# Retention heads of a hybrid decoder step: reordered output projection, earlier splits of a weight unit, later growth of the sample states

## The chip, the cores and the metric

The kernel is one launch on one core of a Trainium2 chip. The metric is the device time in microseconds (us), the median of several executions. One more execution was profiled; all rows below come from that one. The engines are named as in the profile: PE multiplies matrices, PEld is its weight load, DVE works on vectors, ACT evaluates functions, POOL is the general-purpose engine, SP issues DMAs.

## The reference

A trunk of 2 layers works on 592 token columns: 16 meta tokens and 512 prompt tokens of one sequence, and 8 running sequences of 8 tokens each. Cut to what matters here:

```
for each layer:
    xn = rmsnorm(x)
    q, k, v, z_a, x_b, z_b, g_a, g_b = split(xn @ w_in)
    for each of 4 retention heads:                 # dk = 256, dv = 512
        q, k = rope(q), rope(k)
        o = (q k^T * decay) v + (q S) * decay       # prompt: causal; samples: with their own state S
        S_new = gamma^L * S + (k * decay)^T v       # 8 sample states and 1 prompt state, each 256 x 512
        o_a = group_norm(o) * silu(z_a)
    a = o_a @ w_a                                   # summed over the heads
    b = rglru(conv4(x_b)) * silu(z_b) @ w_b
    x = x + (sigmoid(g_a) * a + sigmoid(g_b) * b) @ w_o
y = rmsnorm(x)
```

All inputs and outputs are float32.

## The kernel before

Every engine has its own instruction stream, written out by hand; semaphores order them. A precise float32 product is made of three passes in the fp32r format: each operand is kept as a rounded part (`_hi`) and a remainder (`_lo`), and PE adds hi*hi, lo*hi and hi*lo (`three`, L1558 to L1560; `three_of`, L1623 to L1625, for tiles on the left side that are not weights, and for the values).

**The stream of weights.** The weights come as units of 128 x 1024 numbers (512 KB) in a ring of four slots. SP loads unit u when PE has finished unit u - 4 (`unit_done`). ACT makes `w_hi` of the unit (`split_hi`, L439), DVE makes `w_lo` from it (`split_lo`, L447). In step i of a head both split unit i + 3 of that head (`AHEAD`). Each head has 16 units: 0 to 3 are the columns of q and k, 4 to 7 those of the values, 8 to 11 those of z_a, and 12 to 15 the head's rows of w_a. Two of SP's loads stand behind other work in its queue: unit 10 behind the storing of a block of keys to a scratch buffer, unit 11 behind the same for the values.

**The ring of PSUM banks.** PE writes most of its results (called jobs) into four banks in turn. A job must wait until DVE or ACT has emptied the bank of the job four places earlier (`wait_bank`, `freed`). Jobs are listed in `phases`. Four further banks are outside the ring: two called `sums`, and `v_last` and `o_last`.

**A head** runs on PE in this order: the projections of q and k; the values (`values(0)` to `values(3)`, one call for each of four units; they go to all four banks of the ring, one per block of 128 tokens, and the block of the last 80 tokens to `v_last`); projection 8; the growth of the sample states (`grow`: the product k^T v of two sequences, into two of the banks outside the ring) between the two halves of projection 9 and around the scores; projection 10; the inner products; the prompt's state; four transposes `oT` 0 to 3 of the normalized output of four token blocks; the first half of projection 11; the transposes `oT` 4 of the last token block; the second half of projection 11; and then the product with w_a in 16 jobs `("wa", m)`, for 8 row blocks m and 2 halves of the columns (n = 0, 1). Each of these jobs has 12 matmuls: four parts c, three passes each.

DVE and ACT follow step by step (`i`). In step 7, when the values are done, ACT copies each bank to `vtok_hi` (L744 for the last 80 tokens, then L763 for the four banks), and DVE writes the remainder to `vtok_lo` and frees the bank (L1148, L1171). After that both split unit 10. In step 8 ACT computes a tanh of projection 8 (L733), DVE multiplies (`silu`, L1082), DVE adds the first growth to two states (`grow(0, 0)`, L1060, two instructions; PE's next growth waits for them, because it writes the same two banks), and both split unit 11.

At the end of a head, DVE makes `oa` for the four parts c (`gate`, L1229). ACT rounds it to `oa_hi` (L790). The remainder `oa_lo` of the first three parts over the first 512 tokens is POOL's (L594), the rest is DVE's (`low_oa`, L1225). The last token block is normalized apart (`normalize(4)`, L1219): DVE computes its variance between the gates of c = 0 and c = 1, POOL the power -1/2 of it (`power`, L546). POOL starts on `oa_lo` when this normalization is done:

```
                    power(slice(4, 5), P, hh * 2 + 2)
                    pool.wait_ge(on_ready, hh * 2 + 2)
                    for k in range(3):
```

The second half of `oa` in part 3 is the last thing that is made: it needs the second half of projection 11, ACT's tanh of it, `silu(11, (1,))`, a product, ACT's rounding and DVE's `low_oa(5)`. On PE, the first job with n = 1 waits for it in front of its part c = 3 (`oal_ready`, third value).

After the four heads of a layer the RG-LRU branch, the gates and the output projection follow; the change does not touch them.

Of the kernel before, what the change touches and what calls it, by code (L numbers as in the profile page):

```python
# [39 lines left out]
KT = D_MODEL // P  # L40
# [130 lines left out]
def phases():  # L171
    r = []
    for t in range(4):
        r += halves(("proj", t), 1)
    r += [(("apart", u), 1) for u in range(3)] + [(("v", j), j // 3) for j in range(4)]
    for t in range(8, 11):
        r += halves(("proj", t), 1)
        if t == 9:
            r += [(("score", n), 0) for n in range(len(SCORE_JOBS))]
    r += [(("inner", j), 0) for j in range(4)] + [(("state", c), 0) for c in range(2)]  # L180
    r += [(("oT", c), 0) for c in range(4)] + [((("proj", 11), 0), 0), (("oT", 4), 0), ((("proj", 11), 1), 1)]
    for m in range(0, 8, 2):
        r += [((("wa", m + i), n), n * i) for n in range(2) for i in range(2)]
    l = []
    for g in range(2):
        def apart(which):
            return [(("apart", g, which, gate, n), 0) for gate in range(2) for n in range(2)]

        for t in range(5):
            l += halves(("proj", g, t), 1)  # L190
        l += apart(0) + halves(("proj", g, 5), 1) + apart(1)
        for gate in range(2):
            l += halves(("gate", g, 3, gate), 0)
        l += apart(2)
    four = [x for t in range(4) for x in halves(("proj", t), 1)]
    b = []
    for m in range(8):
        b += halves(("wb", m), (12 * (m + 1)) // 8 - (12 * m) // 8)
    out = {}
    at = (0, 0, 0)  # L200
    for name, passes, units, jobs in (("R", HEADS, 16, r), ("L", 2, 12, l), ("GA", 2, 4, four), ("GB", 2, 4, four),
                                      ("B", 1, 12, b), ("O", 2, 4, four)):
        out[name] = Phase(at, passes, units, jobs)
        at = out[name].after
    return out, at
# [6 lines left out]
def trunk(nc, x_in, w_units, gate_w, packs, final_gain, consts, decay, state_ret,  # L212
# [7 lines left out]
    with ctx:  # L220
# [314 lines left out]
        def _(pool):  # L535
# [13 lines left out]
            for l in range(0, DEPTH):  # L549
# [7 lines left out]
                for h in range(0, HEADS):  # L557
# [31 lines left out]
                    pool.wait_ge(on_ready, hh * 2 + 2)  # L589
# [75 lines left out]
        def _(act):  # L665
# [48 lines left out]
            for l in range(0, DEPTH):  # L714
# [10 lines left out]
                for h in range(0, HEADS):  # L725
# [10 lines left out]
                    for i in range(11):  # L736
# [8 lines left out]
                        if i != 7:  # L745
                            split_hi(act, "R", l, h, i)
# [13 lines left out]
                        if i == 7:  # L760
# [4 lines left out]
                            split_hi(act, "R", l, h, i)  # L765
# [212 lines left out]
        def _(dve):  # L978
# [43 lines left out]
            for l in range(0, DEPTH):  # L1022
# [28 lines left out]
                for h in range(0, HEADS):  # L1051
# [36 lines left out]
                    for i in range(11):  # L1088
# [39 lines left out]
                        elif i == 9:  # L1128
                            silu(i, (0,))
                            grow(0, 1)  # L1130
                            silu(i, (1,))
                        elif i >= 8:
                            silu(i)
                            if i == 8:
                                grow(0, 0)
# [14 lines left out]
                        if i not in (7, 9):  # L1150
# [17 lines left out]
                        if i == 7:  # L1168
# [5 lines left out]
                            split_lo(dve, "R", l, h, i)  # L1174
# [71 lines left out]
                    for c in range(3):  # L1246
# [5 lines left out]
                        if c == 2:  # L1252
# [37 lines left out]
                    for two in range(KT // 2):  # L1290
                        for n, (a, b) in enumerate(cut(l)):
                            for m in (2 * two, 2 * two + 1):
                                name = (("wa", m), n)
                                wait_job(dve, "R", l, h, name)
                                if h == 0:
                                    dve.tensor_copy(acc[:, m, a:b], psum_of("R", name)[:, 0:b - a])\
                                       .then_inc(freed("R", name), 1)
                                else:
                                    dve.tensor_tensor(acc[:, m, a:b], psum_of("R", name)[:, 0:b - a], acc[:, m, a:b],
                                                      ADD).then_inc(freed("R", name), 1)  # L1300
                            if n == 0 and two % 2 == 0:
                                grow_four(two // 2)
                        split_lo(dve, "R", l, h, 12 + two)
# [250 lines left out]
        def _(pe):  # L1554
# [73 lines left out]
            for l in range(0, DEPTH):  # L1628
                for h in range(0, HEADS):
# [158 lines left out]
                    for two in range(KT // 2):  # L1788
                        i = 12 + two
                        wait_unit("R", l, h, i)  # L1790
                        for n, (a, b) in enumerate(cut(l)):
                            for m in (2 * two, 2 * two + 1):
                                name = (("wa", m), n)
                                wait_bank(pe, "R", l, h, name)
                                for c in range(4):
                                    if m == 0 and n == 0 and c < 3:
                                        pe.wait_ge(oapl_ready, hh * 3 + (c + 1))
                                    elif m == 0 and c in (0, 3):
                                        pe.wait_ge(oal_ready, hh * 3 + (1 if n == 0 else 2 if c == 0 else 3))
                                    ins = three(psum_of("R", name)[:, 0:b - a], i % RING, m % 2 * 4 + c,  # L1800
                                                oa_hi[:, c, a:b], oa_lo[:, c, a:b], c == 0, c == 3)
                                done("R", name, ins)
                            if n == 0 and two % 2 == 0:
                                grow_four(two // 2)
# [178 lines left out]
```

## Time and profile before

| | before |
|---|---|
| median of 3 runs | 1956.12 us (1955.78 to 1957.28) |
| the profiled execution, its own time | 1955.78 us |
| its span, from first to last instruction | 1954.0 us |
| granted TensorE clock, mean | 0.997 |
| PE busy | 1928.1 us (99% of the span) |
| PEld busy | 1800.4 us (92%) |
| DVE busy | 1182.3 us (61%) |
| ACT busy | 735.1 us (38%) |
| POOL busy | 239.1 us (12%) |

The profile gives busy time by engine, by groups of instructions, and the idle time in front of each group with what ended it. The timeline lists single instructions of an engine: start, duration, line, tile written and tiles read, and in brackets the idle time before it and what ended that. Where the instructions of one tile are asked for, a row gives the shortest, median and longest duration in ns and the start of the first and the last, and for a DMA the us from its issue to its landing. An instruction of DVE or ACT may begin a little before the modelled end of the one in front of it.

### The profile page before, as it was taken

The page shows a single profiled execution, that of the slowest core. Times are in us where ns is not written, and L with a number is a line of the kernel's source. Part 1 is how long each engine was busy: PE and PEld are TensorE (multiplying, and loading weights), DVE is VectorE, ACT ScalarE, POOL GpSimd, SP SyncE. Part 2 cuts the span into 40 slices and gives each one's busy share as a digit, 9 for nine tenths or more (in the row PEclk, how much of TensorE's full clock was granted, in tenths as well). Part 3 has the DMA queues.
Part 4 walks back from the last instruction along what each step waited for, and adds up shares of the span by engine and source line. Part 5 has one row for each costly group of instructions (what it writes and reads, how often), then busy time and mean ns, then how long its engine had stood idle before and what let it go on. Part 6 is the DMA issues. An engine that isn't in the chain of part 4 may idle for free.

```text
span 1954.0 us, 32049 instructions
## 1 busy us (share of the span) xinstructions
PE 1928.1 (99%) x13176; PEld 1800.4 (92%) x13176; DVE 1182.3 (61%) x2021; ACT 735.1 (38%) x1136; POOL 239.1 (12%) x360
## 2 busy tenths in 40 slices
PE   8999999999999999999999999999999999999997
PEld 7789898898899999999988888988988999999997
DVE  7665565565666887424486655656647668863345
ACT  4332322322326776422333223223223367754222
POOL 1021120120232210000001201202102322000000
PEclk9999999999999999999999999999999999999999
DMA  6334534543453333322245345434534533332222
GB/s 214 123 123 162 166 123 124 171 150 115 133 159 103 99 102 111 124 77 76 87 169 161 119 132 172 159 97 142 189 105 142 162 103 105 101 127 85 82 83 79
DMA packets 105567, 247.00 MB, mean 126 GB/s; under 512 B 10798, under 2 KB 51102, under 8 KB 105038
## 3 DMA queue, kind: packets, MB, share of 16 engines
q1 hardware_dynamic: 78446, 149.74, 24.7%
q0 software_dynamic: 26976, 95.22, 14.6%
q8 instruction: 104, 1.70, 0.4%
q14 instruction: 41, 0.34, 0.1%
HBM read 186.10 MB, written 49.12 MB: 120 GB/s over the span
## 4 chain that ended last, share of the span: by engine, by line
PE 82%; DVE 7%; ACT 5%; ACTq 2%; DVEq 1%; issue 1%; DMA 1%; SPq 0%
PE bank L1558 19%; PE bank L1560 19%; PE bank L1559 19%; PE bank L1623 5%; PE bank L1624 5%; PE bank L1625 5%; PE last L1639 2%; PE last L1623 1%; PE last L1625 1%; PE last L1624 1%; PE sums L1652 1%; DVE ct L1353 1%; DVE rr L1406 1%; ACT ii L860 1%; DVE w_lo L447 1%
## 5 line engine op out<-in xcount | busy, mean ns | idle before, releaser
L1558 PE MATMUL bank<-xn_hi,w_hi 128*128 128x296 f32 (+1 forms) x2432 | 727.3, 299 | 0.0
L1560 PE MATMUL bank<-xn_lo,w_hi 128*128 128x296 f32 (+1 forms) x2432 | 722.8, 297 | 0.0
L1559 PE MATMUL bank<-xn_hi,w_lo 128*128 128x296 f32 (+1 forms) x2432 | 721.8, 297 | 0.0
L1558 PEld LDWEIGHTS bank<-xn_hi,w_hi 128*128 128x128 f32 x2432 | 457.3, 188 | 6.9 <-issue 6.2
L1559 PEld LDWEIGHTS bank<-xn_hi,w_lo 128*128 128x128 f32 x2432 | 457.8, 188 | 0.4
L1560 PEld LDWEIGHTS bank<-xn_lo,w_hi 128*128 128x128 f32 x2432 | 456.8, 188 | 0.0
L447 DVE TENSOR_TENSOR w_lo<-w_raw,w_hi 128x1024 fp32r<-128x1024 f32 x245 | 298.7, 1222 | 183.8 <-ACT w_hi L439 176.7
L439 ACT ACTIVATE w_hi<-w_raw 128x1024 fp32r<-128x1024 f32 x245 | 257.7, 1055 | 358.3 <-DMA w_raw<-in_w_units 353.4
L1558 PE MATMUL bank<-oa_hi,w_hi 128*128 128x296 f32 (+1 forms) x512 | 153.7, 300 | 0.0
L1559 PE MATMUL bank<-oa_hi,w_lo 128*128 128x296 f32 (+1 forms) x512 | 151.9, 297 | 0.0
L1560 PE MATMUL bank<-oa_lo,w_hi 128*128 128x296 f32 (+1 forms) x512 | 151.7, 296 | 0.0
L1558 PE MATMUL bank<-ob_hi,w_hi 128*128 128x296 f32 (+1 forms) x384 | 114.0, 297 | 0.0
L1559 PE MATMUL bank<-ob_hi,w_lo 128*128 128x296 f32 (+1 forms) x384 | 113.9, 297 | 0.0
L1560 PE MATMUL bank<-ob_lo,w_hi 128*128 128x296 f32 (+1 forms) x384 | 113.8, 296 | 0.0
L1623 PE MATMUL bank<-w_hi,xn_hi 128*128 128x512 f32 x256 | 101.6, 397 | 0.0
L1624 PE MATMUL bank<-w_hi,xn_lo 128*128 128x512 f32 x256 | 101.3, 396 | 0.0
L1625 PE MATMUL bank<-w_lo,xn_hi 128*128 128x512 f32 x256 | 101.2, 396 | 0.0
L1558 PEld LDWEIGHTS bank<-oa_hi,w_hi 128*128 128x128 f32 x512 | 96.3, 188 | 3.9 <-issue 3.9
L1559 PEld LDWEIGHTS bank<-oa_hi,w_lo 128*128 128x128 f32 x512 | 96.3, 188 | 0.0
L1560 PEld LDWEIGHTS bank<-oa_lo,w_hi 128*128 128x128 f32 x512 | 96.3, 188 | 0.0
L571 POOL DMA_DIRECT2D out_ret_s<-S x64 | 45.8, 717 | 330.3 <-DVEq L1063 184.3
L1558 PEld LDWEIGHTS bank<-ob_hi,w_hi 128*128 128x128 f32 x384 | 72.2, 188 | 0.0
(272 smaller groups left out, 3004.5 us busy)
## 6 DMA issues: line engine op xcount, KB each, us to landing
w_raw<-in_w_units SPq DMA_DIRECT2D x216, 512.0 KB, 3.6
S<-in_state_ret POOLq DMA_DIRECT2D x64, 512.0 KB, 5.0
out_ret_s<-S POOLq DMA_DIRECT2D x64, 512.0 KB, 6.2
w_raw<-in_w_units SPq DMA_DIRECT2D x64, 256.0 KB, 3.2
vst<-v_scr SPq DMA_DIRECT2D x8, 512.0 KB, 4.0
out_ret_p<-Sp POOLq DMA_DIRECT2D x8, 512.0 KB, 6.1
v_scr<-vtok_hi SPq DMA_DIRECT2D x16, 160.0 KB
dec<-in_decay POOLq DMA_DIRECT2D x9, 264.0 KB, 5.0
```

The source lines that it names most:

```text
L439: act.activation(w_hi[:, n % RING, :], w_raw[:, n % RING, :], ACT.Copy).then_inc(unit_hi, 1)
L447: dve.tensor_tensor(w_lo[:, n % RING, :], w_raw[:, n % RING, :], w_hi[:, n % RING, :].bitcast(f32), SUB).then_inc(unit_lo, 1)
L571: pool.dma_start(dst, S[:, s, :, :]).then_inc(s_out[s], 16)
L860: ins = act.activation(dst[r0:r1, tile, :].rearrange("p (n t) -> p n t", n=2), both[r0:r1, :].rearrange("p (n t) -> p n t", n=2)[:, :, 0:H ...
L1353: dve.scalar_tensor_tensor(ct[:, 0:wide], xpad[:, t, j:j + wide], w(j), ct[:, 0:wide], MUL, ADD)
L1558: pe.matmul(ps, w_hi[:, slot, cols], x_hi, start=first, stop=False)
L1559: pe.matmul(ps, w_lo[:, slot, cols], x_hi, start=False, stop=False)
L1560: return pe.matmul(ps, w_hi[:, slot, cols], x_lo, start=False, stop=last)
L1623: pe.matmul(ps, left_hi, right_hi, start=first, stop=False)
L1624: pe.matmul(ps, left_lo, right_hi, start=False, stop=False)
L1625: return pe.matmul(ps, left_hi, right_lo, start=False, stop=last)
L1639: ins = pe.matmul(o_last[at:at + QUAD, :], qz[:, c, b * QUAD:b * QUAD + QUAD], S[:, s, c, :], start=(n < 4 and c == 0), stop=(n >= 4 and c ...
```

## The change

The change has five parts, all within a retention head.

1. The jobs of w_a are done in another order. Before: for each pair of row blocks, both blocks with n = 0, then both with n = 1. After: each row block with n = 0 and n = 1, then the next. `grow_four` stays behind two jobs in each case.
2. POOL no longer waits for `on_ready` before `oa_lo`.
3. DVE normalizes the last token block after the gate of c = 1, not of c = 2.
4. In step 7, ACT and DVE split unit 10 after the copy of the last 80 tokens' values and before the four copies that free the ring's banks.
5. In step 8, DVE no longer adds the first growth before it splits unit 11; it does so at the beginning of step 9, behind the split.

```diff
@@ phases
-    for m in range(0, 8, 2):
-        r += [((("wa", m + i), n), n * i) for n in range(2) for i in range(2)]
+    for m in range(8):
+        r += halves(("wa", m), m % 2)
@@ gpsimd
                     power(slice(4, 5), P, hh * 2 + 2)
-                    pool.wait_ge(on_ready, hh * 2 + 2)
@@ scalar
-                        if i != 7:
-                            split_hi(act, "R", l, h, i)
+                        split_hi(act, "R", l, h, i)
...
                                 act.activation(vtok_hi[:, j, :], v_bank(j)[:, :], ACT.Copy)\
                                    .then_inc(vth_ready, 1)
-                            split_hi(act, "R", l, h, i)
@@ vector
                         elif i == 9:
+                            grow(0, 0)
                             silu(i, (0,))
                             grow(0, 1)
                             silu(i, (1,))
                         elif i >= 8:
                             silu(i)
-                            if i == 8:
-                                grow(0, 0)
...
-                        if i not in (7, 9):
+                        if i != 9:
                             split_lo(dve, "R", l, h, i)
...
                             dve.drain().then_inc(vtok_ready, 1)
-                            split_lo(dve, "R", l, h, i)
...
-                        if c == 2:
+                        if c == 1:
                             dve.wait_ge(rsd_ready, hh * 2 + 2)
                             normalize(4).then_inc(on_ready, 1)
...
-                    for two in range(KT // 2):
+                    for m in range(KT):
                         for n, (a, b) in enumerate(cut(l)):
-                            for m in (2 * two, 2 * two + 1):
...
-                            if n == 0 and two % 2 == 0:
-                                grow_four(two // 2)
-                        split_lo(dve, "R", l, h, 12 + two)
+                        if m % 2:
+                            split_lo(dve, "R", l, h, 12 + m // 2)
+                        elif m % 4 == 0:
+                            grow_four(m // 4)
@@ tensor
-                    for two in range(KT // 2):
-                        i = 12 + two
-                        wait_unit("R", l, h, i)
+                    for m in range(KT):
+                        i = 12 + m // 2
+                        if m % 2 == 0:
+                            wait_unit("R", l, h, i)
                         for n, (a, b) in enumerate(cut(l)):
-                            for m in (2 * two, 2 * two + 1):
...
-                            if n == 0 and two % 2 == 0:
-                                grow_four(two // 2)
+                        if m % 4 == 0:
+                            grow_four(m // 4)
```

## Rows read from the trace of the kernel before

**Rows 1.** The page, busy time and share of the span.

```profile
PE 1928.1 (99%) x13176; PEld 1800.4 (92%) x13176; DVE 1182.3 (61%) x2021; ACT 735.1 (38%) x1136; POOL 239.1 (12%) x360
```

**Rows 2.** Waits of PE, whole span: us in total, times, longest.

```profile
PE bank L1558 <- DVE w_lo L1007: 9.3, 1, 9.3
PE last L1623 <- DVE xn_lo L1047: 3.9, 4, 1.5
```

**Rows 3.** Load of unit 10 (heads 0, 1, 4, 5): issue, landing.

```profile
L518 SPq DMA_DIRECT2D w_raw<-in_w_units x1: 478/478/478, 70.4 to 70.4; - x1
DMA to landing us min/median/max: 3.7/3.7/3.7
...
L518 SPq DMA_DIRECT2D w_raw<-in_w_units x1: 342/342/342, 205.9 to 205.9; - x1
DMA to landing us min/median/max: 3.6/3.6/3.6
...
L518 SPq DMA_DIRECT2D w_raw<-in_w_units x1: 479/479/479, 1039.9 to 1039.9; - x1
DMA to landing us min/median/max: 3.9/3.9/3.9
...
L518 SPq DMA_DIRECT2D w_raw<-in_w_units x1: 337/337/337, 1173.7 to 1173.7; - x1
DMA to landing us min/median/max: 5.0/5.0/5.0
```

**Rows 4.** Timeline, start of projection 8 (heads 0, 1, 4), DVE's first bank.

```profile
76.40 0.30 PE L1558 MATMUL bank<-xn_hi,w_hi 128*128 128x296 f32 x1
...
212.61 0.30 PE L1558 MATMUL bank<-xn_hi,w_hi 128*128 128x296 f32 x1
...
1045.39 0.29 PE L1558 MATMUL bank<-xn_hi,w_hi 128*128 128x288 f32 x1
...
73.06 0.69 DVE L1171 TENSOR_TENSOR vtok_lo<-bank,vtok_hi 128x512 fp32r<-128x512 f32 x1 [0.70 <-ACT vtok_hi L763]
```

**Rows 5.** Timeline, step 8 and PE's second growth, head 1; last row head 6.

```profile
219.33 0.42 ACT L733 ACTIVATE zz<-bank 128x296 f32<-128x296 f32 x1 [2.84 <-PE bank L1560]
219.64 1.05 ACT L439 ACTIVATE w_hi<-w_raw 128x1024 fp32r<-128x1024 f32 x1
...
220.16 1.40 DVE L1060 SCALAR_TENSOR_TENSOR S<-S,cst,sums 128x512 f32<-128x512 f32 x2
221.47 1.22 DVE L447 TENSOR_TENSOR w_lo<-w_raw,w_hi 128x1024 fp32r<-128x1024 f32 x1
...
223.11 0.50 PE L1652 MATMUL sums<-vst,kst 24*128 24x512 f32 x2
...
1322.99 1.06 ACT L439 ACTIVATE w_hi<-w_raw 128x1024 fp32r<-128x1024 f32 x1 [0.61 <-DMA w_raw<-in_w_units]
```

**Rows 6.** Timeline, end of head 0, POOL, DVE, ACT and PE.

```profile
122.34 0.56 POOL L546 TENSOR_TENSOR rstd_gn<-mv,minus_half 128x1 f32<-128x1 f32 x1 [9.57 <-DVE mv L1213]
124.70 3.79 POOL L594 TENSOR_TENSOR oa_lo<-oa,oa_hi 128x512 fp32r<-128x512 f32 x3 [1.80 <-ACT oa_hi L790]
...
122.18 1.63 DVE L1229 SCALAR_TENSOR_TENSOR oa<-bank,gn_half,zz 128x512 f32<-128x512 f32 x2
123.95 0.55 DVE L1219 TENSOR_SCALAR vo<-vo,mv,rstd_gn 128x512 f32<-128x512 f32 x1
127.98 0.84 DVE L1225 TENSOR_TENSOR oa_lo<-oa,oa_hi 128x296 fp32r<-128x296 f32 x1
130.62 0.47 DVE L1225 TENSOR_TENSOR oa_lo<-oa,oa_hi 128x296 fp32r<-128x296 f32 x1 [0.55 <-ACT oa_hi L790]
...
124.75 0.42 ACT L733 ACTIVATE zz<-bank 128x296 f32<-128x296 f32 x1 [0.22 <-PE bank L1560]
128.52 0.42 ACT L733 ACTIVATE zz<-bank 128x296 f32<-128x296 f32 x1 [0.19 <-PE bank L1560]
...
131.18 0.30 PE L1558 MATMUL bank<-oa_hi,w_hi 128*128 128x296 f32 x1
```

More of the change, by code:

```diff
@@ L1289, in _ @@
                         dve.wait_ge(x_stored, l * 16)
-                    for two in range(KT // 2):
+                    for m in range(KT):
                         for n, (a, b) in enumerate(cut(l)):
-                            for m in (2 * two, 2 * two + 1):
[L1293 to L1300, printed above, removed]
-                            if n == 0 and two % 2 == 0:
-                                grow_four(two // 2)
-                        split_lo(dve, "R", l, h, 12 + two)
+                            name = (("wa", m), n)
+                            wait_job(dve, "R", l, h, name)
+                            if h == 0:
+                                dve.tensor_copy(acc[:, m, a:b], psum_of("R", name)[:, 0:b - a])\
+                                   .then_inc(freed("R", name), 1)
+                            else:
+                                dve.tensor_tensor(acc[:, m, a:b], psum_of("R", name)[:, 0:b - a], acc[:, m, a:b], ADD)\
+                                   .then_inc(freed("R", name), 1)
+                        if m % 2:
+                            split_lo(dve, "R", l, h, 12 + m // 2)
+                        elif m % 4 == 0:
+                            grow_four(m // 4)
                 dve.drain().then_inc(r_done, 1)
@@ L1787, in _ @@
                     project("R", l, h, ("proj", 11), 11, (1,))
-                    for two in range(KT // 2):
-                        i = 12 + two
-                        wait_unit("R", l, h, i)
+                    for m in range(KT):
+                        i = 12 + m // 2
+                        if m % 2 == 0:
+                            wait_unit("R", l, h, i)
                         for n, (a, b) in enumerate(cut(l)):
-                            for m in (2 * two, 2 * two + 1):
[L1793 to L1802, printed above, removed]
-                            if n == 0 and two % 2 == 0:
-                                grow_four(two // 2)
+                            name = (("wa", m), n)
+                            wait_bank(pe, "R", l, h, name)
+                            for c in range(4):
+                                if m == 0 and n == 0 and c < 3:
+                                    pe.wait_ge(oapl_ready, hh * 3 + (c + 1))
+                                elif m == 0 and c in (0, 3):
+                                    pe.wait_ge(oal_ready, hh * 3 + (1 if n == 0 else 2 if c == 0 else 3))
+                                ins = three(psum_of("R", name)[:, 0:b - a], i % RING, m % 2 * 4 + c,
+                                            oa_hi[:, c, a:b], oa_lo[:, c, a:b], c == 0, c == 3)
+                            done("R", name, ins)
+                        if m % 4 == 0:
+                            grow_four(m // 4)
                 pe.wait_ge(grown_free, (l + 1) * (HEADS * 2 * DEC_BATCH) + 1)
```

## The prediction, made before the changed kernel ran

> **What bounds the kernel now.** I read the page's busy times first: PE is busy for 99% of the span, the next engine, DVE, for 61% [rows 1]. Then the waits of PE: the longest is 9.3 us at the very start, the next sum is 3.9 us in four waits for `xn_lo` [rows 2], and no line that the change touches is among them. So PE runs its list almost without a gap, in a fixed order. Any wait that the change adds to PE is added to the time, as nothing later gives it back; and there is next to no wait that it could remove. The question is therefore which of the five parts makes something late for PE. For this I read the timeline at three places of a head. All eight heads show the same pattern with distances equal to some hundredths of a us; only the landings of the weight units differ. Time lies at 0.2 us from a release by another engine to the start of the waiting instruction, as from the end of the normalization at 124.50 (123.95 + 0.55) to POOL's start at 124.70 [rows 6]; I use it for PE too, where the profile shows no such case near, with 0.05 and 0.3 us as bounds.
>
> **Part 4, unit 10 split before the values' banks are freed.** Projection 8 is the next job for the ring, and its first half needs the bank of the first value block. Before, ACT copies it, DVE takes the remainder from 73.06 to 73.75 and the bank is free 2.6 us before PE comes at 76.40 [rows 4]. After, ACT first waits for unit 10 to land, and DVE for ACT. From the landing: ACT starts its split, 1.06 us [rows 5]; DVE splits, 1.22 us, and takes the next instruction about 0.1 us before the modelled end (in head 1 the growth of 1.40 us from 220.16 is followed at 221.47, by 0.09 us early) [rows 5]; its first value bank costs 0.69 us [rows 4]; then 0.2 us to PE. With 0.1 us for the two handovers from DMA to ACT to DVE the chain is 1.06 + 1.13 + 0.69 + 0.2 + 0.1 = 3.2 us from landing to PE.
>
> - Head 0: issued 70.4, landed after 3.7, so 74.1 [rows 3]; PE could start at 77.3 in place of 76.40 [rows 4]: 0.9 us late.
> - Head 4: issued 1039.9, landed 1043.8 [rows 3]; PE at 1047.0 in place of 1045.39 [rows 4]: 1.6 us.
> - Head 1: issued 205.9, landed 209.5 [rows 3]; PE at 212.7 in place of 212.61 [rows 4]: 0.05 to 0.1 us. Heads 2, 3, 6 and 7 have the same distance of 6.7 us from issue to PE and landings of 3.5 or 3.6 us: 0 to 0.1 us each, I take 0.25 us for these five heads together.
> - Head 5 has the distance too, but its landing took 5.0 us [rows 3]: 5.0 + 3.2 - 6.7 = 1.5 us.
>
> The sum is 0.9 + 1.6 + 0.25 + 1.5 = 4.2 us. The landing times set the bounds: all at 3.5 us and the short release give 2 us, all of heads 1 to 7 at 5.0 us give some 12 us. ACT's own copy is no limit: it ends about 0.6 us after its split, before DVE has finished splitting. Behind DVE in this place stand the three other banks; projection 8's second half needs the second one 3.3 us later, and it takes 0.6 us more, so it is hidden. That unit 10 is split earlier brings nothing: it is used only after projection 9 and the scores.
>
> **Part 5, the first growth behind the split of unit 11.** In head 1 PE's second growth runs at 223.11 and writes the banks that DVE's first growth reads [rows 5]. Before, that one ended at 220.16 + 1.40 = 221.56, with 1.5 us to spare. After, the order is ACT's tanh at 219.33, its split at 219.64 to 220.69, DVE's split from 220.73, 1.13 us, and then the growth from 221.87, 1.40 us, to 223.27 [rows 5]; with 0.2 us to PE that is 223.47, so PE waits 0.35 us. In head 6 ACT stood idle for 0.61 us for unit 11 to land [rows 5], which comes on top. In heads 0 and 4 unit 11 is late as well, but by then PE and the tanh are late through part 4, by more than the landing is. The sum is 8 x 0.35 + 0.6 = 3.4 us; the bounds are 8 x 0.2 = 1.6 us and, if unit 11 lands as late as in head 6 everywhere, 8 x 1.0 = 8 us.
>
> **Part 1, the jobs of w_a.** The same products in the same number, and `grow_four` behind the same number of jobs, so the ring and DVE's work keep their times. What moves is the job (0, n = 1): from third, behind a growth, to second place. Its part c = 3 needs DVE's `low_oa(5)`. Before, the fourth part of the second job starts at 131.18, and `low_oa(5)` ends at 130.62 + 0.47 = 131.09 [rows 6]. So with nothing else changed PE would be held for 0 to 0.2 us in each head; the old order had a job and the growth, 2.1 us, as cover. What makes this chain later is now paid in full.
>
> **Parts 2 and 3, POOL without its wait and the early normalization.** After, POOL goes from `power`, which ends at 122.34 + 0.56 = 122.90, straight into `oa_lo` of c = 0, three instructions of 1.26 us [rows 6]. DVE's gate of c = 1 ends at about 122.93, the first of two in 1.63 us, and the normalization follows 0.14 us later, as now behind c = 2 (123.81 to 123.95) [rows 6]: at 123.07. POOL is then 0.1 us ahead and both work on SBUF. What this costs is shown by one row: `low_oa(3)`, with the same shape and work as the 0.47 us of `low_oa(5)`, took 0.84 us from 127.98, while POOL was busy until 124.70 + 3.79 = 128.49 [rows 6]; it ended 0.33 us after POOL. DVE stood still for nearly the whole overlap. Between this and no cost lies the range for the normalization, whose own row shows that 512 numbers took 0.55 us, quicker than the 0.75 us of a gate of that width [rows 6]. I take the held case: it ends at about POOL's 124.2 + 0.4 = 124.6 in place of 123.6, 1.0 us late. The Trainium skill, "SBUF — State Buffer", section "SBUF: two separate sides", says the same in a rule: GpSimd and a VectorE instruction with two SBUF inputs, or in a mode that uses both ports, take one port pair in turn, each for its whole instruction. By it POOL's head start of 0.1 us is what decides; the row of `low_oa(3)` agrees for two inputs, and no row shows it for the normalization.
>
> Held, the delay goes on: the gate of c = 2 ends at 125.3, not at 123.8, 1.5 us later. ACT rounds it and only then takes the tanh of projection 11, which began at 124.75 with 0.22 us idle before it [rows 6]; it moves to 125.9, 1.15 us later. DVE's `silu`, the gate of c = 3, the last block and ACT's rounding of it move by as much, and the second tanh, which had 0.19 us idle and waited for PE [rows 6], moves from 128.52 to about 129.4, by 0.85 us. `low_oa(5)` then ends at 131.9, and PE starts its fourth part at 132.1 in place of 131.18: 0.9 us in each head, 8 x 0.9 = 7.2 us for parts 1, 2 and 3 together. The transposes `oT` 4, which PE reached at 124.55 and could start at 124.8, are within these 0.9 us. Not held, the three parts cost 0 to 0.2 us per head, some 0.8 us in all. POOL's earlier end brings nothing: PE reaches the third part of the first job at about 129.1, POOL ended at 128.49.
>
> **The sum.** 4.2 + 3.4 + 7.2 = 14.8 us on the profiled execution's own 1955.78 us gives 1970.6 us. The median of the runs is 0.34 us above that execution, so I predict 1970.9 us, 0.76% more. A measurement of this kernel tells a change from none from about 0.2%, or 3.9 us.
>
> **The rivals.**
>
> - The normalization is not held (POOL comes later than DVE, or this instruction doesn't collide). For it: POOL is only 0.1 us ahead, by times of 0.1 us grain, and its gates with a PSUM input ran beside POOL undisturbed (`silu` in the same window). Against it: the row of `low_oa(3)`. Time: 4.2 + 3.4 + 0.8 = 8.4 us, 1964.5 us.
> - POOL keeps its turn over two instructions, since its three stand close together (3.79 us for three), and the normalization is held for 2.3 us. For it: no gap between them. Against it: `low_oa(3)` met only the last of the three, so nothing shows it. Each head is 1.26 us later: 14.8 + 10 = 25 us, 1981 us.
> - The loads of units 10 land otherwise, since all transfers shift a little. With the landings of heads 4 and 5 at 3.5 us, part 4 costs 2.3 us less and the time is 1968.6 us; this is inside the range.
> - The other side: PE is held for `on_ready` today. The normalization ends at 124.50 and the transposes come at 124.55, a distance of 0.05 us, which could be a release. The earlier normalization would then give up to 0.2 us per head, 1.6 us, and 1954.5 us. It decides only if parts 4 and 5 cost under 0.2 us per head, that is if DVE frees the value bank 3 us or less after unit 10 lands and the growth takes no place behind the split. Against it: the transposes stand in PE's rhythm, directly behind the matmul in front of them, and PE has no such wait in its list [rows 2].
>
> **How the numbers follow.** My forecast has a chance of 0.52, the first rival 0.27, the second 0.10, the other side 0.04; 0.07 is left for parts 4 and 5 well off their sums in either direction. The forecast's own range is 1967 to 1976 us. To hold 8 in 10 the range takes in the first rival: 1962.5 to 1977 us. Slower by over 0.2% 0.94, within 0.2% 0.05, faster 0.01.
>
> **What would show it.** In the profile of the changed kernel: PE's waits name DVE's L1171 (`vtok_lo`) in front of projection 8, long in heads 0, 4 and 5, near nothing elsewhere; DVE's L1060 in front of the second growth, 0.3 to 0.4 us in each head; and DVE's `low_oa(5)`, L1225, in front of a matmul with `oa_hi`, 0.9 us in each head. The normalization of the last block takes 1.5 us in place of 0.55, and `low_oa(3)` 0.47 us in place of 0.84. If it takes 0.55 us, the first rival is right. If PE shows no wait for L1171, the chain of part 4 is wrong, and if the span grows by more than PE's named waits, I have missed a place.

## The result and the profile after

The changed kernel takes 1966.9 us (median of 5 runs, 1965.73 to 1969.67), the kernel before 1955.78 us on the same chip (5 runs, 1955.32 to 1957.28). The medians are 11.1 us apart. The ratio of the runs is 1.0062, with a 95% interval of 1.0051 to 1.0074, which is 12 us. The profiled execution has a span of 1965.1 us, 11.1 us more than before, and the granted clock is 0.998.

The page of the changed kernel, busy times:

```profile
PE 1931.5 (98%) x13176; PEld 1799.6 (92%) x13176; DVE 1184.6 (60%) x2021; ACT 732.0 (37%) x1136; POOL 240.9 (12%) x360
```

The instructions are the same in number, and no engine has more work worth speaking of [rows 1]. What is new stands in the list of PE's waits (us in total, times, longest):

```profile
PE bank L1553 <- DVE w_lo L1004: 8.9, 1, 8.9
...
PE bank L1553 <- DVE vtok_lo L1167: 3.1, 3, 1.3
PE sums L1647 <- DVE S L1057: 2.6, 6, 1.0
...
PE bank L1553 <- DVE oa_lo L1220: 0.9, 4, 0.2
```

The first row was there before [rows 2]. The other three are the three places of the prediction: `vtok_lo` is the first value bank in front of projection 8, `S` the first growth in front of the second, `oa_lo` the last remainder in front of the fourth part of a w_a job. This list counts only what is left when the modelled end of the matmul in front is taken off; the whole of a wait is seen in the distance between two starts.

**Step 7.** Timeline of the changed kernel, head 0, ACT, DVE and PE; the last row is the start of projection 8 in head 5:

```profile
69.23 0.59 ACT L743 ACTIVATE vtok_hi<-last 80x512 fp32r<-80x512 f32 x1 [4.24 <-PE last L1620]
72.63 1.06 ACT L439 ACTIVATE w_hi<-w_raw 128x1024 fp32r<-128x1024 f32 x1 [2.80 <-DMA w_raw<-in_w_units]
73.60 2.04 ACT L761 ACTIVATE vtok_hi<-bank 128x512 fp32r<-128x512 f32 x4
...
73.72 1.23 DVE L447 TENSOR_TENSOR w_lo<-w_raw,w_hi 128x1024 fp32r<-128x1024 f32 x1 [3.18 <-ACT w_hi L439]
74.87 2.48 DVE L1167 TENSOR_TENSOR vtok_lo<-bank,vtok_hi 128x512 fp32r<-128x512 f32 x4
...
74.36 0.40 PE L1620 MATMUL bank<-w_lo,xn_hi 128*128 128x512 f32 x1
75.70 0.38 PE L1553 MATMUL bank<-xn_hi,w_hi 128*128 128x296 f32 x1 [0.94 <-DVE vtok_lo L1167]
...
1188.21 0.37 PE L1553 MATMUL bank<-xn_hi,w_hi 128*128 128x288 f32 x1 [1.30 <-DVE vtok_lo L1167]
```

ACT stands idle for 2.8 us until unit 10 lands, with a value bank ready to be copied; then everything follows in the new order, and PE starts projection 8 3.1 us after the landing. The last value matmul starts at 74.36 and projection 8 at 75.70, a distance of 1.34 us; it is 0.23 us where nothing is late. In heads 4 and 5 the distances are 1.27 and 1.69 us, in the five others 0.23 or 0.24. What a distance has above 0.23 us is the cost: part 4 costs 1.1 + 1.0 + 1.5 = 3.6 us in this execution.

**Step 8.** The same for head 1; the last two rows, one of ACT and one of PE, are of head 2:

```profile
219.59 0.42 ACT L732 ACTIVATE zz<-bank 128x296 f32<-128x296 f32 x1 [2.84 <-PE bank L1555]
219.91 1.05 ACT L439 ACTIVATE w_hi<-w_raw 128x1024 fp32r<-128x1024 f32 x1
...
220.99 1.23 DVE L447 TENSOR_TENSOR w_lo<-w_raw,w_hi 128x1024 fp32r<-128x1024 f32 x1 [0.48 <-ACT w_hi L439]
222.14 1.40 DVE L1057 SCALAR_TENSOR_TENSOR S<-S,cst,sums 128x512 f32<-128x512 f32 x2
...
223.59 0.50 PE L1647 MATMUL sums<-vst,kst 24*128 24x512 f32 x2 [0.15 <-DVE S L1057]
...
357.98 1.06 ACT L439 ACTIVATE w_hi<-w_raw 128x1024 fp32r<-128x1024 f32 x1 [0.83 <-DMA w_raw<-in_w_units]
...
361.67 0.50 PE L1647 MATMUL sums<-vst,kst 24*128 24x512 f32 x2 [0.98 <-DVE S L1057]
```

In head 1 the growth ends at 222.14 + 1.40 = 223.54 and PE goes on at 223.59. In head 2 unit 11 lands late, ACT is idle for 0.83 us, and PE waits 0.98 us; before, it was head 6 where it landed late [rows 5]. The distance from the matmul in front of PE's second growth to it is 0.45 us in heads 0, 1 and 3, 0.51 us in head 5 and 1.28 us in head 2, against 0.22 or 0.23 us before. In heads 4, 6 and 7 it is 0.70 to 0.76 us: there too ACT had to wait a little for unit 11 after its tanh, and PE goes on 3.7 us after the landing, as in head 2. Summed over eight heads the excess is 3.5 us, of which 2.0 us is the new order (0.22 us in each head of the first layer, 0.29 in the second) and 1.5 us the landings.

**The end of a head.** Head 0 of the changed kernel, POOL, DVE, ACT and PE:

```profile
121.86 0.56 POOL L546 TENSOR_TENSOR rstd_gn<-mv,minus_half 128x1 f32<-128x1 f32 x1 [9.57 <-DVE mv L1208]
122.39 2.71 POOL L593 TENSOR_TENSOR oa_lo<-oa,oa_hi 128x512 fp32r<-128x512 f32 x2
...
122.58 1.38 DVE L1214 TENSOR_SCALAR vo<-vo,mv,rstd_gn 128x512 f32<-128x512 f32 x1
123.88 0.74 DVE L1224 SCALAR_TENSOR_TENSOR oa<-bank,gn_half,zz 128x512 f32<-128x512 f32 x1
...
130.73 0.47 DVE L1220 TENSOR_TENSOR oa_lo<-oa,oa_hi 128x296 fp32r<-128x296 f32 x1 [0.55 <-ACT oa_hi L787]
...
125.24 0.40 ACT L732 ACTIVATE zz<-bank 128x296 f32<-128x296 f32 x1
...
124.06 0.61 PE L1780 MATMUL bank<-cst,vo 128*128 128x128 f32 x4
124.76 0.38 PE L1553 MATMUL bank<-xn_hi,w_hi 128*128 128x296 f32 x1
...
131.25 0.41 PE L1553 MATMUL bank<-oa_hi,w_hi 128*128 128x296 f32 x1
```

POOL starts its first remainder 0.19 us before DVE's normalization, and the normalization takes 1.38 us in place of 0.55 [rows 6]. It ends 0.28 us after POOL's first remainder, and POOL's second remainder takes 1.46 us in place of 1.29. PE is late twice. The last remainder ends at 130.73 + 0.47 = 131.20 and PE starts its fourth part at 131.25, 0.41 us behind the matmul in front of it (0.5 us in the second layer, 0.13 without a wait). The other place was not in the prediction: between the starts of the transposes `oT` 4 (124.06) and of the second half of projection 11 (124.76) lie 0.70 us. In the kernel before it was 0.41 us:

```profile
124.56 0.66 PE L1785 MATMUL bank<-cst,vo 128*128 128x128 f32 x4
124.97 0.38 PE L1558 MATMUL bank<-xn_hi,w_hi 128*128 128x296 f32 x1
```

That half of projection 11 goes into the bank of the transposes of c = 2, which the gate of c = 2 empties at 123.88 + 0.74 = 124.62. This gate stands behind the held normalization. So the end of a head costs 8 x 0.29 us there and 4 x 0.28 + 4 x 0.37 us in front of the fourth part; behind that second stop the next matmul also comes after 0.24 us in place of 0.14. Together that is some 5.7 us.

The three sums, 3.6 + 3.5 + 5.7 = 12.8 us, are 1.7 us more than the growth of the span. The beginning makes the difference: the last value matmul of head 0 starts at 74.36 here, and 1.8 us later in the kernel before (0.23 us in front of the 76.40 of [rows 4]); the change has nothing in front of it. Most of it is TensorE's clock. In the profiled execution of the kernel before, the granted clock was at its lower level for 3.4 us from 53.1 us on, which cost PE 1.6 us; in that of the changed kernel it was not. The stretch in the kernel before and in the changed kernel (us, PE, PEld, DVE, ACT and POOL busy, granted clock, DMA share, GB/s):

```profile
53.20:56.40 3.20, 3.20 (x9) 2.50 (x8) 2.57 (x4) 1.23 (x2) 0.00 (x0) 0.50 0.00 0
...
53.20:56.40 3.20, 3.20 (x16) 2.59 (x14) 2.57 (x5) 0.98 (x3) 0.00 (x0) 1.00 0.00 0
```

So the difference of these two spans understates what the change costs by 1.7 us.

### The profile page after: what moved, and what is told of

The parts are those of the page before. It is cut to its first block, busy times and chain, and to the rows that moved or that the text cites. A ratio compares the mean times of both kernels' runs of the same rounds, so it can differ in the third digit from the quotient of the medians.

```text
span 1965.1 us, 32049 instructions
## 1 busy us (share of the span) xinstructions
PE 1931.5 (98%) x13176; PEld 1799.6 (92%) x13176; DVE 1184.6 (60%) x2021; ACT 732.0 (37%) x1136; POOL 240.9 (12%) x360
## 4 chain that ended last, share of the span: by engine, by line
PE 68%; DVE 11%; ACT 7%; issue 4%; DMA 3%; DVEq 2%; ACTq 2%; SPq 1%; POOL 0%; POOLq 0%
PE bank L1553 17%; PE bank L1555 17%; PE bank L1554 17%; PE bank L1618 4%; PE bank L1620 4%; PE bank L1619 4%; DMA w_raw<-in_w_units 2%; DVE w_lo L447 1%; ACT w_hi L439 1%; DVE ct L1348 1%; PE last L1634 1%; PE sums L1647 1%; PE last L1618 1%; DVE rr L1401 1%; PE last L1620 1%
## 5 line engine op out<-in xcount | busy, mean ns | idle before, releaser
L1079 DVE SCALAR_TENSOR_TENSOR zz<-zz,bank 128x296 f32<-128x296 f32 (+1 forms) x64 | 29.3, 457 | 80.2 <-ACT zz L732 79.9
```

The costliest lines, as they stand in the source:

```text
L1079: dve.scalar_tensor_tensor(zz[:, i - 8, a:b], zz[:, i - 8, a:b], 1.0, psum_of("R", name)[:, 0:b - a], ADD, MUL)\
```

## The experiments

**Each part alone.** Three kernels split the change, a fourth takes the order of the w_a jobs by itself. They ran on one chip.

`e1_split10`, part 4 alone:

```diff
-                        if i != 7:
-                            split_hi(act, "R", l, h, i)
+                        split_hi(act, "R", l, h, i)
...                                                          # behind the four banks
-                            split_hi(act, "R", l, h, i)
...
-                        if i not in (7, 9):
+                        if i != 9:
                             split_lo(dve, "R", l, h, i)
...                                                          # behind the four banks
-                            split_lo(dve, "R", l, h, i)
```

> The kernel before with part 4 alone: unit 10 is split before the four value banks are freed. My theory (PE waits in front of projection 8 for the first value bank, because DVE stands in its queue behind unit 10): 4 us slower in all, with PE waits for DVE's vtok_lo of about 1.1 us in head 0, 1 to 1.6 us in head 4 and in any head where unit 10 lands after 5 us, and none elsewhere. Rival (the waits of the changed kernel at this place come from its other parts, through the ring or the loads): no more than 1 us slower and no wait for vtok_lo.

Measured: 1959.2 us, before 1956.47 us, ratio 1.0015 (1.0006 to 1.0024), 2.9 us. In the waits of PE, DVE's remainder of the value bank stands as in the changed kernel:

```profile
PE bank L1555 <- DVE vtok_lo L1169: 2.9, 3, 1.9
```

Projection 8 starts at 76.73 in head 0, 2.0 us late, 0.9 us late in head 4, 0.5 us in head 5, where the landing took 4.1 us this time, and 0.2 us in head 6, where it took 3.8 us. In the heads with a landing of 3.5 or 3.6 us and 6.7 us from issue to PE there is no wait. Head 0 is later than expected, and not by its landing: unit 10 was issued at 69.91, only 4.8 us before PE was due, against 5.8 us in the changed kernel, and landed after 3.7 us. The theory holds; the size follows the issue and the landing from execution to execution.

`e2_growth`, part 5 alone:

```diff
                         elif i == 9:
+                            grow(0, 0)
                             silu(i, (0,))
...
-                            if i == 8:
-                                grow(0, 0)
```

> The kernel before with part 5 alone: DVE splits unit 11 before it adds the first growth. My theory: PE waits in front of its second growth for DVE's first one, 0.2 to 0.5 us in most heads, and about 0.9 us in head 0 and 1.2 us in head 4, where unit 11 lands late and part 4 is not there to cover it; 4 to 5 us in all. Rival (unit 11's landing has no part in it, only the order of DVE counts): the same 0.2 to 0.5 us in all heads, 2 to 3 us in all.

Measured: 1960.78 us, ratio 1.0021 (1.0012 to 1.0031), 4.1 us.

```profile
PE sums L1651 <- DVE S L1060: 3.4, 6, 1.1
```

PE's second growth is 0.2 to 0.3 us late in five heads, 0.9 us in head 0, 1.1 us in head 4 and 1.0 us in head 6. So the landing of unit 11 counts where the delay of part 4 does not stand in front of it, as the theory had it. In the changed kernel the same waits are 0.2 us in head 0 and 0.5 us in head 4: the parts overlap there.

`e3_end`, parts 1, 2 and 3, and `e4_order`, part 1 alone (the diffs are those of the change).

> The kernel before with parts 1, 2 and 3: new order of the jobs of w_a, POOL without its wait, normalization behind the gate of c = 1. My theory: DVE's normalization of the last block is held by POOL's first remainder and takes 1.4 us in place of 0.55; PE pays twice, 0.3 us in front of the second half of projection 11 (bank of the transposes of c = 2) and 0.3 to 0.4 us in front of the fourth part of the second job of w_a; 5 us in all. Rival (the three parts cost only what my first sum had without the hold): 1 us or less.

> The kernel before with part 1 alone: the jobs of w_a in the order of the changed kernel. My theory: the last remainder of oa ends just before PE wants it, so PE waits less than 0.1 us per head, 0 to 0.6 us in all, within the noise. Rival (the old order was a cover that is already needed, so the order by itself costs): 0.2 us or more per head, 1.6 us or more in all, with a PE wait for low_oa in each head.

Measured: `e3_end` 1961.86 us, ratio 1.0028 (1.0018 to 1.0037), 5.5 us; `e4_order` 1956.37 us, ratio 1.0 (0.9991 to 1.0009). In the first one the normalization takes 1.38 us again, and PE's weight load waits in all eight heads (the row below); in the second one PE has no wait for `oa_lo`:

```profile
PEld bank L1557 <- DVE oa_lo L1224: 3.2, 8, 0.5
```

The three groups add up: 0.15% + 0.21% + 0.28% = 0.64%, the change has 0.62%. The new order costs nothing by itself.

**What holds the normalization.** `e5_end_old_order` has parts 2 and 3 with the old order, `e7_order_norm` has parts 1 and 3 with POOL's wait kept (`pool.wait_ge(on_ready, hh * 2 + 2)` back in its place).

> The kernel before with parts 2 and 3 but the old order of the jobs of w_a. My theory: the normalization takes 1.4 us, PE waits 0.3 us in front of the second half of projection 11, and the later wait is covered by the old order; 2 to 2.5 us in all. Rival (the two waits are one delay that PE meets wherever it comes first): 5 us, as with the new order.

> The kernel before with parts 1 and 3, POOL's wait kept. My theory: without POOL beside it the normalization takes 0.55 us in its new place too; 0 to 1 us slower than before, from a small wait for the last remainder. Rival (the place of the normalization, not POOL, costs the time): 3 us or more.

Measured: `e5_end_old_order` 1958.11 us, before 1956.46 us, ratio 1.0008 (0.9999 to 1.0017); `e7_order_norm` 1956.48 us, ratio 1.0 (0.9991 to 1.0008). With the old order the second of PE's two waits is gone and the first one stays, 0.29 us in each head in the trace; the time of the runs, 1.6 us, is just inside the noise (the interval takes in 1), and below the 2 us that were expected. With POOL's wait kept, the normalization is as quick as before in its new place. The groups of 40 normalizations, `e5_end_old_order` above and `e7_order_norm` below (busy us, mean ns):

```profile
L1218 DVE TENSOR_SCALAR vo<-vo,mv,rstd_gn 128x512 f32<-128x512 f32 x40 | 26.3, 709 | 10.4 <-POOL rstd_gn L546 9.3
```

```profile
L1219 DVE TENSOR_SCALAR vo<-vo,mv,rstd_gn 128x512 f32<-128x512 f32 x40 | 19.7, 545 | 10.4 <-POOL rstd_gn L546 9.3
```

So POOL is the cause, not the place: (26.3 - 19.7) / 8 = 0.83 us for each held normalization.

The trace of `e7_order_norm` also shows something small that the earlier place gives. From the start of the transposes `oT` 4, which read what the normalization writes, to the second half of projection 11 it takes 0.35 us in all eight heads, as in the three other kernels whose early normalization is not held by a remainder (`e9_dve_first`, `e10_dec_only`, `e12_repaired`). In the kernel before, and in the kernels with the normalization in its old place, it takes 0.41 us. That is 0.5 us for eight heads, which the times of the runs cannot tell from nothing.

**Who starts first.** Two kernels reverse the order of the two starts. In `e9_dve_first` POOL waits for the gate of c = 1, which puts it 0.1 us behind DVE; in `e6_end_dec_first` it issues the load of the next decay table before its remainders. Both have parts 1, 2 and 3.

```diff
                     power(slice(4, 5), P, hh * 2 + 2)
+                    pool.wait_ge(oa_ready, hh * PARTS + 2)                                       # e9_dve_first
...
                     power(slice(4, 5), P, hh * 2 + 2)
+                    pool.dma_start(dec[:, :], decay[ds(h + 1, 1)]...).then_inc(dec_in, 16)       # e6_end_dec_first
...
-                    pool.dma_start(dec[:, :], decay[ds(h + 1, 1)]...).then_inc(dec_in, 16)       # e6_end_dec_first
```

> The kernel before with parts 1, 2 and 3, and POOL starts its remainders only when DVE's gate of c = 1 is written, so that it comes about 0.1 us behind DVE's normalization. Theory of turns (who starts first keeps the SBUF port for its whole instruction): the normalization takes 0.55 us, POOL's first remainder takes some 0.3 us longer, 0 to 1 us slower than before in all. Rival (POOL wins whenever both are there): the normalization takes 1.4 us or more and the time is 5 us above before.

> The kernel before with parts 1, 2 and 3, and POOL issues the load of the next decay table (some 0.6 us) before its three remainders of oa in place of behind them, so that DVE's normalization starts first. My theory (POOL and DVE take turns by the instruction, and who starts first goes on): the normalization takes 0.55 us, gate c = 2 frees its bank in time, 0 to 1 us slower than before. Rival (both are slowed wherever they overlap, whoever starts first): the normalization takes 1 us or more and the cost stays at 3 us or more. Other rival (the normalization is slow in its new place whatever POOL does): 1.4 us, 5 us in all.

Measured: `e9_dve_first` 1955.66 us, before 1955.88 us, ratio 0.9996 (0.9987 to 1.0005). Its timeline, head 0, POOL and DVE:

```profile
121.63 4.08 POOL L594 TENSOR_TENSOR oa_lo<-oa,oa_hi 128x512 fp32r<-128x512 f32 x3 [0.27 <-DVEq L1249]
...
121.52 0.55 DVE L1219 TENSOR_SCALAR vo<-vo,mv,rstd_gn 128x512 f32<-128x512 f32 x1
```

DVE is 0.11 us ahead and is not held; now POOL pays, 4.08 us for its three remainders in place of 3.79 [rows 6]. So between these two instructions a head start of 0.1 or 0.2 us decides who waits.

`e6_end_dec_first` missed its expectation widely: 1984.96 us, before 1956.46 us, ratio 1.0144 (1.013 to 1.0158), 28.5 us. Timeline, head 0, POOL and DVE:

```profile
123.08 0.61 POOL L589 DMA_DIRECT2D dec<-in_decay  x1
123.71 2.50 POOL L594 TENSOR_TENSOR oa_lo<-oa,oa_hi 128x512 fp32r<-128x512 f32 x2
...
123.28 3.23 DVE L1218 TENSOR_SCALAR vo<-vo,mv,rstd_gn 128x512 f32<-128x512 f32 x1
```

The normalization, dispatched 0.2 us after POOL's issue of the DMA and 0.4 us before POOL's first remainder, ends at 126.51, 0.30 us after the second remainder. A reading that fits is that DVE was not first here: the issue of the DMA on POOL had taken the turn already, and the remainders behind it kept it. The Trainium skill, "SBUF — State Buffer", section "Who interferes with whom", has both halves: `tensor_scalar` can run in a mode with two ports, which cannot run beside a GpSimd instruction, and the writing of DMA descriptors by GpSimd needs a port too; whoever issues first keeps the pair for its instruction. The runs agree for a pair of single instructions; no run here shows which mode the normalization ran in, and that several instructions of POOL in a row go first is not in the rule.

`e10_dec_only` and `e11_dec_one` take this apart: in the first one only the DMA's issue runs beside the normalization, in the second one the issue and one remainder, then POOL waits. Both have parts 1 and 3; `e11_dec_one` has part 2 with the wait put behind the first remainder. The issue is moved, as in `e6_end_dec_first`.

```diff
+                    pool.dma_start(dec[:, :], decay[ds(h + 1, 1)]...).then_inc(dec_in, 16)
-                    pool.wait_ge(on_ready, hh * 2 + 2)           # kept in e10_dec_only
                     for k in range(3):
                         what = (slice(None),) + pieces(l)[k]
+                        if k == 1:                               # e11_dec_one alone
+                            pool.wait_ge(on_ready, hh * 2 + 2)
```

> The kernel before with parts 1 and 3 and POOL's wait kept, and POOL's issue of the decay table's load put in front of that wait. Only this issue runs beside the normalization now, no remainder. If POOL's issue of a DMA holds DVE as a remainder does: the normalization takes 0.7 to 0.9 us, it ends 0.3 us behind the issue, and the time is within 1 us of before. If it does not: 0.55 us, and the 3.2 us that the normalization took with the issue and two remainders behind it have another cause.

> The kernel before with parts 1, 2 and 3; POOL issues the decay table's load, does one remainder, waits for the normalization, and does the other two. Where the issue and two remainders stood in a row, the normalization took 3.2 us. If POOL keeps its turn while its instructions stand close together: 1.9 to 2.1 us here, ended by the wait. If the wait of the normalization is one stretch that does not depend on how many follow: 3 us, or a standstill. PE stops for 0.8 us per head instead of 1.8, TensorE keeps its clock, and the time is 10 to 16 us above before, not 28.

Measured: `e10_dec_only` 1956.21 us, before 1955.88 us, ratio 1.0001 (0.9992 to 1.001); `e11_dec_one` 1967.62 us, ratio 1.0057 (1.0044 to 1.0071), 11.7 us. The two timelines, head 0:

```profile
122.69 0.61 POOL L589 DMA_DIRECT2D dec<-in_decay  x1
...
122.90 0.63 DVE L1219 TENSOR_SCALAR vo<-vo,mv,rstd_gn 128x512 f32<-128x512 f32 x1
```

```profile
122.02 0.61 POOL L589 DMA_DIRECT2D dec<-in_decay  x1
122.65 1.29 POOL L596 TENSOR_TENSOR oa_lo<-oa,oa_hi 128x512 fp32r<-128x512 f32 x1
...
122.23 2.01 DVE L1220 TENSOR_SCALAR vo<-vo,mv,rstd_gn 128x512 f32<-128x512 f32 x1
```

With the issue alone the normalization ends 0.23 us behind it and takes 0.63 us (0.62 to 0.65 in the eight heads) in place of 0.55. That is between the two expected values; it speaks for a hold, of which 0.08 us shows because the normalization needs most of the time anyway. With one remainder behind the issue it takes 2.01 us and ends 0.30 us after that remainder, with two 3.23 us. The hold grows by one remainder each time, which speaks for turns that POOL keeps. But in the changed kernel the normalization came through between the first and the second remainder, though these stood close together as well. Why it did there and not here is open.

**Repairs.** `e8_split10_second` moves the split of unit 10 behind the first value bank and changes nothing else of the kernel before; `e12_repaired` adds to it the new order of the jobs and the early normalization, with POOL's wait kept and the first growth in its old place.

```diff
                                 act.activation(vtok_hi[:, j, :], v_bank(j)[:, :], ACT.Copy)\
                                    .then_inc(vth_ready, 1)
-                            split_hi(act, "R", l, h, i)
+                                if j == VALUE_ORDER[1]:
+                                    split_hi(act, "R", l, h, i)
...
                                                   SUB).then_inc(freed("R", ("v", j)), 1)
+                                if j == VALUE_ORDER[1]:
+                                    split_lo(dve, "R", l, h, i)
                             dve.drain().then_inc(vtok_ready, 1)
-                            split_lo(dve, "R", l, h, i)
```

> The kernel before with unit 10 split on ACT and DVE behind the first of the four value banks, not in front of it. My theory (only the first bank is wanted at once, the second one 3.3 us later): no PE wait for vtok_lo and the time of before, within 1 us. Rival (any split of unit 10 that early holds up the values' copies and PE with them): 2 to 4 us slower.

> The changed kernel with its three costs taken back and nothing else: POOL's wait kept, unit 10 split behind the first of the four value banks, the first growth in front of the split of unit 11; the new order of the jobs of w_a and the early normalization stay. If the three places are all that the change costs: the time of the kernel before, within 1 us. If the new order or the early normalization cost or gain something of their own in this company: 1.5 us or more to either side.

Measured: `e8_split10_second` 1955.46 us, before 1956.46 us, ratio 0.9997 (0.9988 to 1.0006); `e12_repaired` 1956.56 us, before 1955.88 us, ratio 0.9998 (0.9989 to 1.0007). DVE of the former in head 0, and the start of projection 8, which comes 0.23 us behind the last value matmul:

```profile
71.64 0.69 DVE L1172 TENSOR_TENSOR vtok_lo<-bank,vtok_hi 128x512 fp32r<-128x512 f32 x1 [0.70 <-ACT vtok_hi L763]
73.89 1.23 DVE L447 TENSOR_TENSOR w_lo<-w_raw,w_hi 128x1024 fp32r<-128x1024 f32 x1 [1.56 <-ACT w_hi L439]
75.03 1.88 DVE L1172 TENSOR_TENSOR vtok_lo<-bank,vtok_hi 128x512 fp32r<-128x512 f32 x3
...
74.98 0.30 PE L1560 MATMUL bank<-xn_hi,w_hi 128*128 128x296 f32 x1
```

One bank taken before the split is enough: the second one is freed at 75.7, after PE has begun projection 8, and PE does not miss it. Neither kernel beats the one before by more than the noise, so at these places there was at most 0.1% to win, and 0.6% to lose.

## Why the prediction was right, point by point

- PE has no gap to spare, so every added wait is added to the time: right. The excess distances on PE, 12.8 us, make up the growth of the span from the last value matmul of head 0 on, 12.9 us.
- Part 4: predicted 4.2 us, 3.6 us in the trace and 2.9 us alone. The heads were the right ones, 0, 4 and 5 (0.9, 1.6 and 1.5 us predicted, 1.1, 1.0 and 1.5 us measured), and the chain of 3.2 us from landing to PE measured 3.1 us. The error is in the issues and landings, which differ from execution to execution: in head 4 unit 10 was issued 5.5 us before PE was due in the kernel before and 5.8 us in the changed one, and in head 5 the landing took 5.1 us in the changed kernel and 4.1 us in `e1_split10`.
- Part 5: predicted 3.4 us, 3.5 us in the trace, 4.1 us alone. That the sum is so near is partly luck. The wait without a late landing is 0.22 us in the first layer and 0.29 us in the second, not 0.35, since PE goes on 0.05 us after the growth ends and not 0.2; and unit 11 landed late in four heads, for 1.5 us, not in one for 0.6. That part 4 covers the late unit 11 in heads 0 and 4 was right in the main: without it the two cost 2.0 us, with it 0.7.
- Part 1: nothing by itself, as the sum had it, and cover for what else is late: right (`e4_order`, `e5_end_old_order`).
- Parts 2 and 3: the held normalization was right in kind, and that POOL's start, 0.19 us ahead, decides. The terms were too large: 7.2 us predicted with part 1, 5.7 us in the trace, 5.5 us alone. The hold is 0.83 us, not 1.0. The chain behind it moved the last remainder by 0.6 us, not 0.85: I had not taken off the 0.36 us that `low_oa(3)` and `low_oa(4)` win when POOL is done before them (1.15 us for both before, 0.79 us after, by the timelines). And PE went on 0.05 us after the release where I had taken 0.2.
- The step that failed: "The transposes `oT` 4 ... are within these 0.9 us". They were in time. PE met the delay one job later, in front of the second half of projection 11, because of the bank that the gate of c = 2 empties. I had followed the data of this gate and not its bank. It did not hurt the sum much, since with the new order PE's two waits are parts of one delay: 0.7 us in each head, 0.9 predicted. With the old order (`e5_end_old_order`) this place alone remains, where the prediction's account has nothing.
- The first rival (not held) is refuted by the 1.38 us. The second one (POOL keeps its turn over two instructions) did not happen in the changed kernel, but it did in `e6_end_dec_first`. The other side is refuted by `e7_order_norm` as a price that could count: the earlier normalization gives 0.06 us in each head by the trace, not 0.2, and nothing that the runs can show.
- The number: 14.8 us predicted, 11 to 12 measured. The terms are 2.0 us too large, 1.5 at the end of a head and 0.6 in part 4; the rest of the distance to the 11.1 us between the spans is the clock at the beginning of the kernel before, which the prediction took along in its 1955.78 us.

## What to carry to other kernels

When an engine's queue is reordered, follow both what an instruction writes and what it frees: a bank or slot that is emptied behind a wait for a DMA holds up the engine that fills it next, and one item taken before the wait can be enough. An instruction that is ready early is no gain if nobody waits for it, and its place in the queue is then paid by all that stand behind it. A wait that looks needless may keep two engines apart that share a port: look at which of the two starts first before it is taken out, and count the issue of a DMA as an instruction too.

## What the runs showed of the hardware that I had not expected

A short stop of PE can cost nearly as much again through its clock. In `e6_end_dec_first` each head stops PE for 1.8 us. Before the stop of head 0 the clock was at its upper level, and 1.7 us after PE went on, it fell to the lower one for 3.4 us, in which the matmuls of 296 columns came every 0.25 us in place of 0.136. Busy time by stretch, before the stop, behind it, in the slow stretch and after it (columns as above):

```profile
120.00:124.60 4.60, 4.60 (x39) 4.60 (x38) 3.76 (x6) 1.83 (x3) 2.01 (x3) 1.00 0.07 9
126.50:128.20 1.70, 1.54 (x10) 1.33 (x11) 1.12 (x3) 0.94 (x2) 0.14 (x1) 1.00 0.00 0
128.40:131.40 3.00, 3.00 (x14) 3.00 (x14) 2.63 (x12) 0.86 (x2) 1.64 (x2) 0.50 0.27 105
132.00:136.00 4.00, 4.00 (x31) 3.59 (x29) 2.02 (x4) 2.06 (x4) 0.00 (x0) 1.00 0.39 131
```

A clock of 0.50 is 1.2 GHz, 1.00 is 2.4 GHz. Some 14 matmuls at 0.11 us more are 1.6 us. Six of the eight heads show this; in heads 4 and 6, after the same stop, the clock stays at 1.00, and the way from the transposes `oT` 4 to the first w_a job takes 4.0 us in place of 5.5 to 5.6. Why these two were spared is open. So about 10 of the 28.5 us are clock, by this estimate, and most of the rest is stop. `e1_split10` shows the same once, behind its stop of 2.0 us in head 0: the granted clock is 0.50 from 77.5 to 80.9, and the way from projection 8 to the second growth is 1.5 us longer. Stops of 0.6 us (`e11_dec_one`, clock 1.00 in the same stretch) and of 1.5 us (the changed kernel, head 5) had no such sequel. The same stop can go either way: at 50 us both the kernel before and the changed kernel have a stop of PE of 1.5 us, and the former had the slow stretch at 53 us behind it, the latter did not.
